# Two norms' shift sums as one rounded product each, a convolution's norm sums by high and low parts

## What is computed

```python
def layer_norm(x, g, b):
    mu = jnp.mean(xf, axis=-1, keepdims=True)
    var = jnp.mean(jnp.square(xf - mu), axis=-1, keepdims=True)
    y = (xf - mu) * lax.rsqrt(var + LN_EPS)
    ...
def mixer_conformer_conv(a, b, gate, conv_w, conv_b, ln_g, ln_b):
    y = a * jax.nn.sigmoid(b)
    ...
        feature_group_count=W_B) + conv_b
    y = layer_norm(y, ln_g, ln_b)
    return jax.nn.silu(y) * jax.nn.silu(gate)
```

## Time and profile before

| | |
|---|---|
| median of three runs | 1629.76 us |
| profiled execution, first to last instruction | 1627.6 us |
| TensorE busy | 99% of the span, granted clock 0.998 in the mean |
| VectorE / ScalarE / GpSimd busy | 71% / 39% / 44% |
| TensorE in the 40 slices | 9 tenths or more in 39, 7 in the last |

### The profile page before, as it was taken

One profiled execution on the slowest core, in us unless ns is written; L12 is line 12 of the kernel. 1 busy time (PEld: TensorE's weight loads), 2 busy tenths in 40 slices (PEclk: granted clock), 3 DMA queues, 4 the chain that ended last, 5 costly groups with the idle time before them and its releaser, 6 DMA issues. The chain is left out here.

```text
span 1627.6 us, 21084 instructions
## 1 busy us (share of the span) xinstructions
PE 1605.5 (99%) x7644; PEld 1307.1 (80%) x7644; DVE 1148.0 (71%) x1652; ACT 629.2 (39%) x1014; POOL 708.9 (44%) x390
## 2 busy tenths in 40 slices
PE   9999999999999999999999999999999999999997
PEld 5888888888877888888888788887878888877785
DVE  6441788862499777777776766787996995299557
ACT  6221444521165444444443222255563112258214
POOL 2444111154515233332225678581556654454552
PEclk9999999999999999999999999999999999999999
DMA  5521101032523443333439996314201111110012
GB/s 198 81 61 40 40 27 39 27 134 86 197 88 138 172 156 149 149 142 143 164 152 347 395 409 255 142 38 156 65 27 39 39 52 52 39 53 23 18 39 104
DMA packets 54854, 190.31 MB, mean 117 GB/s; under 512 B 5889, under 2 KB 8002, under 8 KB 54122
## 3 DMA queue, kind: packets, MB, share of 16 engines
q1 hardware_dynamic: 49650, 172.05, 29.0%
q10 hardware_dynamic: 5112, 17.04, 3.6%
HBM read 134.02 MB, written 55.05 MB: 116 GB/s over the span
## 5 line engine op out<-in xcount | busy, mean ns | idle before, releaser
L637 POOL TENSOR_SCALAR w_hi<-raw 128x1024 fp32r<-128x1024 f32 x48 | 143.8, 2995 | 265.7 <-PE G L838 215.4
L838 PE MATMUL G<-B_hi,w_hi 128*128 128x512 f32 x480 | 149.4, 393 | 0.2 <-ACT yb L1960 0.2
L838 PE MATMUL G<-B_lo,w_hi 128*128 128x512 f32 x480 | 148.0, 389 | 0.0
L838 PE MATMUL G<-B_hi,w_lo 128*128 128x512 f32 x480 | 147.8, 389 | 0.0
L838 PE MATMUL G<-A_hi,w_hi 128*128 128x512 f32 x432 | 138.3, 401 | 0.0
L681 POOL TENSOR_TENSOR S<-fraw 128x512 f32<-128x512 f32 x33 | 47.0, 1425 | 202.2 <-DVE ring_lo L2449 194.3
L838 PE MATMUL G<-A_lo,w_hi 128*128 128x512 f32 x432 | 133.5, 390 | 0.0
L838 PE MATMUL G<-A_hi,w_lo 128*128 128x512 f32 x432 | 133.3, 390 | 0.0
L639 POOL TENSOR_TENSOR w_lo<-raw,w_hi 128x1024 fp32r<-128x1024 f32 x48 | 126.9, 2643 | 4.0
L1685 ACT ACTIVATE ring_hi<-S 128x512 fp32r<-128x512 f32 x132 | 82.1, 628 | 111.7 <-PE U L1151 34.0
L1113 PE MATMUL G<-X_hi,ring_hi 128*128 128x512 f32 x308 | 120.0, 390 | 2.2 <-DVE sf L2464 1.1
(11 more groups left out here) (448 smaller groups left out, 3815.5 us busy)
## 6 DMA issues: line engine op xcount, KB each, us to landing
raw<-in_weights SPq DMA_DIRECT2D x72, 512.0 KB, 3.6
hid_spill<-hst SPq DMA_DIRECT2D x72, 512.0 KB, 2.6
fraw<-in_weights SPq DMA_DIRECT2D x66, 512.0 KB, 4.5
Dc<-hid_spill SPq DMA_DIRECT2D x56, 512.0 KB, 12.8
Dc<-hid_spill ACTq DMA_DIRECT2D x14, 512.0 KB, 7.8
h_spill<-h SPq DMA_DIRECT2D x8, 512.0 KB, 6.8
pj_spill<-pj_out SPq DMA_DIRECT2D x8, 512.0 KB, 2.7
h<-h_spill SPq DMA_DIRECT2D x8, 512.0 KB, 6.1
```

The lines of the kernel that those rows point to most:

```text
L637: pool.tensor_scalar(hi, raw[:, u, :], 1.0, None, ALU.mult).then_inc(w_hi_done, 1)
L838: mm = pe.matmul(G[g][:, b * HT:(b + 1) * HT], w, x[:, k, b * HT:(b + 1) * HT], start=s0, stop=s1)
```

## The change

The shift sums read float32r: `ones256` and the sums of the first two tiles are written as float32r (`acc2r`, `acc3r`, the same memory as `acc2` and `acc3`). The running sum is no longer made from the shift but from the two centred tiles, in `first_parts`. For the convolution's norm each of the two sums takes four float32r matmuls on a high part `t2_hi` (made by ScalarE from `t1`) and a low part `t1_lo` (made by VectorE, `t1` less `t2_hi`), with a float32r matrix of ones; ScalarE makes the high part ahead of reading `vn`, VectorE makes the low part behind `bn_aggr`. Semaphores of the first block are merged into two (`decay_in`, `decay_made`), with the same waits.

```diff
-        ones256 = at("ones256", 44, [P, P])
+        ones256 = at("ones256", 44, [P, P], F32R)
+        acc2r = at("acc2r", 40, [P, T], F32R)
...
+        t1_lo, t2_hi = at("t1_lo", 60, [P, T], F32R), at("t2_hi", 56, [P, T], F32R)
+        ones_r = at("ones_r", 52, [P, P], F32R)
...
-            gemm(0, S_PLE + 3, C_PLE // 2 + 2, 0, A3_hi, A3_lo, before={0: lambda: shift_sum(2, acc2, ones256)})
+            gemm(0, S_PLE + 3, C_PLE // 2 + 2, 0, A3_hi, A3_lo, before={0: lambda: shift_sum(2, acc2r, ones256)})
...
+            def conv_sums(n, dst):
+
+                pe.wait_ge(clo_done, n)
+                for src, start in ((t2_hi, True), (t1_lo, False)):
+                    for b in range(2):
+                        mm = pe.matmul(dst[:, hs(b)], ones_r[:, :], src[:, hs(b)], start=start, stop=not start)
+                mm.then_inc(cstat, 1)
...
-            pe.wait_ge(csum_done, 1)
             pe.wait_ge(avtok_done, 2)
-            sums(U01, t1, cstat)
+            conv_sums(1, U01)
             with pe.Fori(7, 9) as i:
                 pair(2 * i + S_IN2, i + a2)
-            pe.wait_ge(csum_done, 2)
-            sums(U23, t1, cstat)
+            conv_sums(2, U23)
             pair(S_IN2 + 18, a2 + 9)
...
-            gemm(1, S_OUT2 + 2, C_OUT2 // 2 + 1, 1, B_hi, B_lo, before={5: lambda: shift_sum(PARTS5 + 2, acc3, ones256)})
+            gemm(1, S_OUT2 + 2, C_OUT2 // 2 + 1, 1, B_hi, B_lo, before={5: lambda: shift_sum(PARTS5 + 2, acc3r, ones256)})
...
+            def conv_hi(n):
+
+                act.wait_ge(csum_done, n)
+                act.activation(t2_hi[:, :], t1[:, :], ACT.Copy).then_inc(chi_done, 1)
+
             act.wait_ge(avt_done, 1)
-            act.wait_ge(csum_done, 1)
+            conv_hi(1)
             for j in range(2):
                 act.activation(vn[:, :, j * P:(j + 1) * P], (U01, U23)[j].rearrange("p (c n) -> p c n", c=NBLK), ACT.Copy).then_inc(avtok_done, 1)
...
                 act.activation(dst[:, :], co[:, j, :], ACT.Square).then_inc(csq, 1)
+            conv_hi(2)
             for n in range(14, 16):
...
-            def unshift(total, shift):
-
-                dve.scalar_tensor_tensor(total[:, :], shift, -2.0, total[:, :], ALU.mult, ALU.add).then_inc(part_done, 1)
+            def first_parts(total, n):
+
+                dve.wait_ge(d_done, n)
+                dve.tensor_tensor(total[:, :], h[:, 0, :], h[:, 1, :], ALU.add).then_inc(part_done, 1)
...
             centre(0, E3 + 1)
             read_gate(2)
-            dve.wait_ge(part_done, 2)
-            unshift(acc2, U01)
             centre(1, E3 + 2)
             g2 = gated(2)
+            first_parts(acc2, 2)
...
+            dve.tensor_copy(ones_r[:, :], ones[:, :])
             tick.wait()
             dve.tensor_tensor(t1[:, :], co[:, 0, :], co[:, 1, :], ALU.add).then_inc(csum_done, 1)
...
             ins.then_inc(bag_done, 1)
+            def conv_lo(n):
+
+                dve.wait_ge(chi_done, n)
+                dve.tensor_tensor(t1_lo[:, :], t1[:, :], f(t2_hi[:, :]), ALU.subtract).then_inc(clo_done, 1)
+
+            conv_lo(1)
             dve.wait_ge(vrt_done, 1)
...
             dve.tensor_tensor(t1[:, :], t1[:, :], t2[:, :], ALU.add).then_inc(csum_done, 1)
+            conv_lo(2)
             dve.wait_ge(crt, 1)
...
             centre2(0), centre2(1)
-            dve.wait_ge(part_done, PARTS5 + 2)
-            unshift(acc3, U01)
+            first_parts(acc3, D5 + 2)
```

More of the change, by code:

```diff
@@ L277, in build @@
         Vt = at("Vt", 56, [P, NBLK, P])
-        acc3 = at("acc3", 32, [P, T])
+        acc3, acc3r = at("acc3", 32, [P, T]), at("acc3r", 32, [P, T], F32R)
         rows0, rows1 = at("rows0", 24, [P, 2, HT]), at("rows1", 184, [P, 2, HT])
         t1, t2 = at("t1", 60, [P, T]), at("t2", 56, [P, T])
+        t1_lo, t2_hi = at("t1_lo", 60, [P, T], F32R), at("t2_hi", 56, [P, T], F32R)
+        ones_r = at("ones_r", 52, [P, P], F32R)
         avT = at("avT", 188, [P, 2, T])
@@ L340, in build @@
         f_done, fv_done, ones_done, low_done = map(sem, ("f_done", "fv_done", "ones_done", "low_done"))
-        logit_done, sp_done, la_done, cum_done, vtr_done, V_done, sg_done = map(
-            sem, ("logit_done", "sp_done", "la_done", "cum_done", "vtr_done", "V_done", "sg_done"))
+        decay_in, decay_made, vtr_done, V_done, sg_done = map(
+            sem, ("decay_in", "decay_made", "vtr_done", "V_done", "sg_done"))
         D_done, E_done, K_done, kdt_done, kdT_done, lvl_done, lvl_used = map(
@@ L363, in build @@
         fin_done, b_read = sem("fin_done"), sem("b_read")
+        chi_done, clo_done = sem("chi_done"), sem("clo_done")
         hg_done = sem("hg_done")
@@ L947, in _ @@
                                start=True, stop=True)
-            mm.then_inc(logit_done, 1)
+            mm.then_inc(decay_in, 1)
             gemm(1, S_VG, 2, 1, A_hi, A_lo)
@@ L957, in _ @@
             gemm(0, S_VG + 1, 3, 0, A_hi, A_lo)
-            pe.wait_ge(la_done, 1)
+            pe.wait_ge(decay_made, 2)
             for j in range(QK_TILES):
@@ L963, in _ @@
                                    start=True, stop=True)
-            mm.then_inc(cum_done, 1)
+            mm.then_inc(decay_in, 1)
             gemm(1, S_VG + 2, 3, 1, A_hi, A_lo)
@@ L1545, in _ @@
             sp_flat = sp_t[:, :, :].rearrange("p a n -> p (a n)")
-            act.wait_ge(logit_done, 1)
+            act.wait_ge(decay_in, 1)
             tick(act.activation(sp_flat, logits, ACT.Abs))
@@ L1550, in _ @@
             tick.wait()
-            act.activation(sp_flat, sp_flat, ACT.Ln, bias=col("one")).then_inc(sp_done, 1)
+            act.activation(sp_flat, sp_flat, ACT.Ln, bias=col("one")).then_inc(decay_made, 1)
             def gate_silu(j):
@@ L1578, in _ @@
             gate_silu(0)
-            act.wait_ge(cum_done, 1)
+            act.wait_ge(decay_in, 2)
             act.activation(bT[:, :, :].rearrange("p a n -> p (a n)"), logits, ACT.Copy).then_inc(out_free, 1)
@@ L2211, in _ @@
                 dve.scalar_tensor_tensor(qT[:, j, :], G[s % 2][:, :], DK ** -0.5, R[:, :], ALU.mult, ALU.mult).then_inc(acc_free[s % 2], 1)
-            dve.wait_ge(sp_done, 1)
+            dve.wait_ge(decay_made, 1)
             dve.scalar_tensor_tensor(la[:, :, :].rearrange("p a n -> p (a n)"), U[:, :, :].rearrange("p a n -> p (a n)"), 0.0,
-                                     sp_t[:, :, :].rearrange("p a n -> p (a n)"), ALU.min, ALU.subtract).then_inc(la_done, 1)
+                                     sp_t[:, :, :].rearrange("p a n -> p (a n)"), ALU.min, ALU.subtract).then_inc(decay_made, 1)
             read_out(S_VG, 1, vT[:, :])
@@ L2631, in _ @@
             tick.wait(first)
-            dve.scalar_tensor_tensor(acc2[:, :], h[:, 1, :], col("lnf", 1), acc2[:, :], ALU.mult, ALU.add).then_inc(part_done, 1)
+            dve.scalar_tensor_tensor(acc2r[:, :], h[:, 1, :], col("lnf", 1), acc2[:, :], ALU.mult, ALU.add).then_inc(part_done, 1)
             dve.wait_ge(stat_done, 4)
@@ L2983, in _ @@
             summed(0), summed(1)
-            dve.tensor_tensor(acc3[:, :], h[:, 0, :], h[:, 1, :], ALU.add).then_inc(part_done, 1)
+            dve.tensor_tensor(acc3r[:, :], h[:, 0, :], h[:, 1, :], ALU.add).then_inc(part_done, 1)
             dve.wait_ge(stat_done, N2.stat)
             centre2(0), centre2(1)
-            dve.wait_ge(part_done, PARTS5 + 2)
-            unshift(acc3, U01)
+            first_parts(acc3, D5 + 2)
             dve.wait_ge(sq_done, E5 + 2)
```

## The result

The changed kernel takes 1631.9 us (median of 19 runs, 1630.46 to 1632.95), the kernel before 1628.87 us in 19 runs beside it: a ratio of 1.0017, 95% interval 1.0011 to 1.0023, or 2.8 us more (1.0017 times the time before; the two medians lie 3.0 us apart). The forecast was 2.9 us more. Three executions far off all others (1841.12 and 2062.33 us of the kernel before, 5735.60 us of e2) are left out of the ratios. The profiled execution has a span of 1629.3 us.

A forecast was written before the change was run, and what follows sets the result against it. TensorE was taken as the bound: −1.31 (first shift) + 4.85 (convolution's first sum with its wait) − 0.86 (second sum) − 1.31 (second shift) + 1.5 (clock) = +2.9 us, so 1632.6 us, range 1630.1 to 1635.0.

The forecast's parts named there:

- TensorE bounds, what it saves comes off and what it waits for is added: Whole kernel: TensorE is busy 1605.5 of 1627.6 us, so its saved work shortens the time and its waits lengthen it.
- Shift sums, −1.31 us each: At the first and last norms, float32r shift sums save 1.31 us each on TensorE, arriving in full.
- The convolution's start: Sign in the changed kernel's timeline: the convolution starts 1.3 us earlier than 1243.70.
- The convolution's products, 0.91 for 1.83 and 1.77: Convolution's norm: four float32r matmuls take 0.91 us per sum, saving 0.92 and 0.86 us.
- The wait, 5.77 us: Convolution's first sum: TensorE stands idle 5.77 us until VectorE's low part is there.
- The chain of steps: Ahead of the convolution's first sum: ones copy, channel sum, high part, `vn` reads, statistics, low part, hand-over at 1356.28.
- No wait at the second sum: Convolution's second sum: low part there at 1376, TensorE asks after 1400, leaving only the 0.86 us gain.
- the squares' sum: VectorE's step ahead of the convolution's second sum, starting at 1369.79 before, would be some 2.4 us later.
- The clock, 1.5 us between 0 and 3.05: TensorE's clock falls in the gap at the convolution's first sum, costing 1.5 us, the middle of two bounds.
- Sum +2.9 us: Whole kernel: +1.37 us from savings and wait, +1.5 for the clock, giving 1632.6 us.
- The dearer rival: Longer gap or dearer clock at the convolution's first sum: 1634.2 us, up to 1635.5; chance 0.19.
- the forecast's own case: Whole kernel: the gap with a clock cost, reaching from 1631.6 to 1634.0 us; chance 0.51.

The follow-up runs named there:

- e2: Changed kernel with both norms' shift sums back in float32 and the running sum made from the shift; convolution's part kept: 1.0032 of the kernel before.
- e1: Changed kernel with the convolution's part put back to float32, both float32r shift sums kept: 0.9987 of the kernel before.
- e6: Changed kernel with the convolution's part and the last norm's shift sum back in float32; first norm's shift sum in float32r: 0.9988 of the kernel before.
- e5: Changed kernel with the convolution's first sum moved one gemm later on TensorE only: 0.9986 of the kernel before.
- e3: Changed kernel with 18 useless matmuls put into TensorE's gap ahead of the convolution's first sum: 1.0012 of the kernel before.
- e10: Changed kernel with the gap filled by 18 useless matmuls, run again beside the changed kernel: 1629.83 us, 1.0007 of the kernel before.
- e9: The changed kernel itself, run again beside the version with the filled gap: 1632.32 us, 1.0019 of the kernel before.
- e8: Changed kernel with 9 useless matmuls put into TensorE's gap instead of 18: median 1630.8 us, 1.0011 of the kernel before.
- e11: Changed kernel with 3 useless matmuls put into TensorE's gap: 1632.39 us, 1.0022 of the kernel before.
- e7: Changed kernel with the convolution's first sum one gemm later and ScalarE's read of slot 12 moved earlier: 1624.86 us, 0.9972 of the kernel before.

## Why the prediction was right, point by point

- *TensorE bounds, what it saves comes off and what it waits for is added.* Right: the ledger's sum lies in the measured ratio's interval in all twelve rows, though these intervals are some 1 to 2 us wide to each side.
- *Shift sums, −1.31 us each.* Right, D shows it for the last and A of e1 and e6 for the first: 1.31, 1.31 and 1.29 us. That the first arrives in full had been read from the 3.05 us that VectorE waited, and it did. The convolution's start, which the prediction had named as a sign, is at 1241.33 instead of 1243.70, and counted from the first shift sum 1.23 us earlier.
- *The convolution's products, 0.91 for 1.83 and 1.77.* Right: C is shorter by 0.86, and e5, where no wait stands ahead of the first sum, has the full 0.92. In e3 and e10 B is shorter by 0.78 only, since behind a wait the first pair takes 0.57 us instead of 0.45 (1353.64 to 1354.21 in e3).
- *The wait, 5.77 us.* 5.61 measured. The chain of steps was the right one, in the right order; the copy of the ones cost 0.13 instead of 0.2 us, and `bn_aggr` gave way to the low part after 0.56 instead of 0.65 us.
- *No wait at the second sum.* Right: of the waits of TensorE none stands there, and C is shorter by the product's whole saving. The way there was mis-sized without consequence: the squares' sum on VectorE was to be some 2.4 us later. It starts 238.29 us behind the first shift sum and had 238.67 before; with the 1.31 us that all else came forward, it is 0.9 us later.
- *The clock, 1.5 us between 0 and 3.05.* Right in kind, and 1.56 us in the first profile (3.37 − 1.81), of which 0.14 is the slower start behind any wait; by B against e3 it is 1.4, and 2.2 in e9's profile, which has the usual mean clock. This was the weakest term, taken as the middle of two far bounds, and the agreement to a tenth is luck; the two profiles of this one kernel lie 0.8 us apart, half of the term. The Trainium skill's rule ("TensorE: Matmul & The Clock Gate", "Part 1: The HAM clock gate"), that an idle TensorE goes back to the throttled state, agrees with the changed kernel's trace (1.00 in the window from 1352 to 1353 and 0.50 from 1354 on, behind 5.4 us without work). In e8 and e11 the fall came 0.65 and 0.13 us after work had been taken up again.
- *Sum +2.9 us.* +2.8 measured, +2.81 in the ledger: −1.31 + 5.61 + 0.91 − 1.83 + 1.56 = +4.94 for A and B, which measure +4.98, then −0.86 and −1.31. With the price of e9's profile the ledger is +3.37, so that part of this agreement is luck too.
- *The dearer rival's limits.* They do not fit each other: it was to decide from a gap of 7.2 us or from 1.9 us for the clock. The first goes with 1634.0 us, the upper end of the forecast's own case, the second with 1633.0. For 1633.0 the gap would be 6.2 us. The gap of 5.6 us is below both.

What was not foreseen came with the experiments: that a sum moved out of a wait uncovers the next one (e5, and by 0.4 us e7), and how much the clock's price differs between executions.

## What to carry to other kernels

When a product on the busiest engine is made cheaper by preparing its operands elsewhere, write down the new steps in each engine's order with the durations of the old trace: here 0.9 us were saved and 5.6 us of waiting bought, because one subtraction stood behind statistics that waited for a third engine. Look for idle time of the preparing engine just ahead of it; moving one line there, or the product one gemm later together with the read that it uncovers, turned +2.8 us into −3.4 and −4.0 in the ledger. Count a gap of some microseconds on TensorE as dearer than its length.

## What the runs showed of the hardware

- The granted clock fell at 1353.44 in the changed kernel (5.2 us after its last matmul had ended), at 1352.10 in the same kernel's second profile (3.2 us after it), in e8 0.65 us after work had resumed, behind an idle stretch of 2.18 us, and in e11 0.13 us after it, behind 3.56 us. At the kernel's end it had been 3.8 us.
- It was low for 3.4 us in one profile of the changed kernel (1353.44 to 1356.86) and for 6.8 us in the other (1352.10 to 1358.94), though the gap was the same. In such a stretch a pair of 512-column float32r matmuls costs 0.85 us instead of 0.45.
- In e2's profile, and in none of the other twelve, the clock was also low near the kernel's start, from 11.7 to 15.1 us (0.83 in the window from 11 to 12, then 0.50, 0.97 from 15 to 16). TensorE was at work when it fell; its last idle stretch, of 1.88 us, had ended at 9.93. The ledger does not hold this stretch, and e2's first shift sum is the latest of all, at 1132.05.
- Filling the gap with 18 useless matmuls made the kernel 2.5 us faster (1629.83 against 1632.32 us, side by side).
- TensorE takes 0.57 us instead of 0.45 for the first pair behind a short wait at the full clock (e3, also 0.54 in e7 behind an idle time of 0.15 us).
